# A two-block transformer kernel: a root of squares moved from the memory queries into a column factor, the opening put in another order, three sums regrouped

## What is computed

```
h    = rms_norm(x, mix_pre);   proj = h @ w_in            # two latents cq (384 wide), ckv (256 wide) among others
q    = rms_norm(cq, g_cq) @ w_uq;   kv = rms_norm(ckv, g_ckv) @ w_ukv
x    = x + rms_norm(mix @ w_mix_out, mix_post)
h    = rms_norm(x, mem_pre);   mem_n = rms_norm(mem, mem_kv)   # mem: 256 tokens, the same in both layers
q    = h @ w_q;   k, v = mem_n @ w_kv
p    = softmax(q @ k.T / 16)                              # 4 heads of 256 columns
x    = x + rms_norm((p @ v) @ w_o, mem_post)
x    = x + rms_norm(conv_ffn(rms_norm(x, ffn_pre)), ffn_post)
```

## Time and profile before

| what | us |
| --- | --- |
| median of 3 runs (2935.09 to 2936.07) | 2935.51 |
| the profiled execution | 2936.66 |
| its span, first to last instruction | 2934.9 |
| PE busy | 2823.6 |
| DVE busy | 1645.3 |
| ACT busy | 1175.8 |

### The profile page before, as it was taken

How to read it: one execution, slowest core, us unless ns; L and a number is a source line. 1 busy time by engine, 2 the same in 40 slices (tenths; PEclk the granted TensorE clock), 3 DMA queues, 4 the chain that set the end, 5 groups by cost and what they waited for, 6 DMA issues and landing times. The chain is left out here.

```text
span 2934.9 us, 35880 instructions
## 1 busy us (share of the span) xinstructions
PE 2823.6 (96%) x14736; PEld 2269.3 (77%) x14736; DVE 1645.3 (56%) x2278; ACT 1175.8 (40%) x1727; POOL 287.3 (10%) x249
## 2 busy tenths in 40 slices
PE   7999999999999999999999999999999999999998
PEld 3888777678878888786687878888786778788886
DVE  4467256676645443567753466653668663566643
ACT  3732434442243332434643343333435643443332
POOL 0110024310001110001200001100002101011100
PEclk8999999999999999999999999999999999999999
DMA  6200210045422222220032222232220132222231
GB/s 238 72 30 1 94 44 30 30 139 191 148 74 99 100 100 89 99 82 29 30 115 87 72 86 95 92 110 101 72 72 15 58 115 72 72 100 88 100 101 58
DMA packets 46003, 249.52 MB, mean 85 GB/s; under 512 B 5136, under 2 KB 7312, under 8 KB 19344
## 3 DMA queue, kind: packets, MB, share of 16 engines
q1 hardware_dynamic: 45840, 247.23, 24.5%
HBM read 245.11 MB, written 2.10 MB: 84 GB/s over the span
## 5 line engine op out<-in xcount | busy, mean ns | idle before, releaser
L271 DVE TENSOR_TENSOR ring_lo<-ring,ring_hi 128x2048 fp32r<-128x2048 f32 x199 | 457.2, 2298 | 552.9 <-ACT ring_hi L264 552.7
L322 PE MATMUL bank<-h_hi,ring_hi 128*128 128x512 f32 x1360 | 544.3, 400 | 12.5 <-PEq L380 8.7
L264 ACT ACTIVATE ring_hi<-ring 128x2048 fp32r<-128x2048 f32 x199 | 379.5, 1908 | 384.6 <-PE bank L322 356.6
L322 PE MATMUL bank<-h_hi,ring_lo 128*128 128x512 f32 x1360 | 531.5, 391 | 0.0
L1629 PE MATMUL bank<-h_hi,ring_hi 128*128 128x512 f32 x960 | 374.3, 390 | 0.0
L1633 PE MATMUL bank<-h_hi,ring_lo 128*128 128x512 f32 x960 | 373.5, 389 | 0.0
L1632 PE MATMUL bank<-h_lo,ring_hi 128*128 128x512 f32 x960 | 373.4, 389 | 0.0
L322 PEld LDWEIGHTS bank<-h_hi,ring_hi 128*128 128x128 f32 x1360 | 256.5, 189 | 70.3 <-DVE ring_lo L271 8.4
L322 PEld LDWEIGHTS bank<-h_hi,ring_lo 128*128 128x128 f32 x1360 | 256.3, 188 | 54.6
L322 PE MATMUL bank<-h_lo,ring_hi 128*128 128x512 f32 x624 | 244.9, 393 | 0.0
L1632 PEld LDWEIGHTS bank<-h_lo,ring_hi 128*128 128x128 f32 x960 | 180.2, 188 | 38.0 <-issue 0.5
(11 more groups left out here) (465 smaller groups left out, 4899.5 us busy)
## 6 DMA issues: line engine op xcount, KB each, us to landing
ring<-in_stream SPq DMA_DIRECT2D x199, 1024.0 KB, 4.9
mod_w<-in_stream SPq DMA_DIRECT2D x64, 256.0 KB, 3.6
ring<-in_stream SPq DMA_DIRECT2D x7, 512.0 KB, 4.1
ring<-in_stream SPq DMA_DIRECT2D x10, 256.0 KB, 4.2
h_spare<-in_stream SPq DMA_DIRECT2D x2, 1024.0 KB, 9.3
xT<-in_xT SPq DMA_DIRECT2D x2, 1024.0 KB, 18.1
xT<-in_xT SPq DMA_DIRECT2D x1, 2048.0 KB, 9.5
memT<-in_memT SPq DMA_DIRECT2D x2, 1024.0 KB, 5.3
```

Of the source, the lines that this page charges most:

```text
L264: nc.scalar.activation(self.slab_hi(slab + j), self.slab(slab + j), ACT.Copy).then_inc(slab_rounded, 1)
L271: nc.vector.tensor_tensor(lower, self.slab(slab + j), self.slab_hi(slab + j).bitcast(F32), ALU.subtract)\
L322: ins = nc.tensor.matmul(out, lhsT, rhs, start=start and w is w_hi and x is x_hi, stop=stop and w is w_lo)
```

## The change

It does six things in one kernel.

1. Opening: PE adds up `acc` and turns first, and sums the squares of x between the two halves of the third group. The slab roundings move: ACT rounds the first slab before the root of x, DVE halves it before it waits for `mod`. The second slab is rounded in the next block, behind the third rounded tile, and halved at tile 5, not 4.
2. Front: 5 useless products, not 18.
3. Latents: DVE adds the squares (three additions), PE does two products, not five.
4. Memory squares and their root are made in the first layer alone and kept in `mem_root`.
5. `mix_and_memory`: `h` is x times the gain, without the root. ACT makes `h_hi` from x, DVE `h_lo`; the squares go to `raw`; PE's eight sums are gone.
6. `memory_attention`: DVE adds the eight squares, PE sums them behind the first query tile, ACT takes the root, PE turns it into a column (four products of one column), and the exponential has it as a factor per partition. DVE multiplies each maximum by it.

```diff
@@ modulation: act @@
+                ws.round_to(act, WHOLE_SLABS, RING_SLABS)
                 act.wait_ge(x_summed.sem, x_summed.at(1))
                 root_of_mean(act, x_scales[:, 0, :], bank[:, 5, :])
                 row(2)
-                ws.round_to(act, WHOLE_SLABS + 1, RING_SLABS)
@@ front @@
-                linear("front", tiles, banks=6, busy=18, ...)
+                linear("front", tiles, banks=6, busy=5, ...)
@@ latents @@
+                    def low_totals(dve):
+                        for lo, hi, _, _ in latents:
+                            for n in range(lo + 1, hi):
+                                dve.wait_ge(low_squared.sem, low_squared.at(n + 1))
+                                if n > lo + 1:
+                                    dve.drain()
+                                last = nc.vector.tensor_tensor(low_square[lo], low_square[lo], low_square[n], ALU.add)
+                            last.then_inc(low_added.sem, 1)
@@ mix_and_memory: pe @@
-                for j in range(5):
+                for j in range(KT):
                     key_tile(j)
-                next_sums(range(4))
-                for j in range(5, KT - 1):
-                    key_tile(j)
-                next_sums(range(4, KT))
-                key_tile(KT - 1)
@@ mix_and_memory: act @@
+                for n in range(KT):
+                    key_out(n)
+                    round_h(n)
+                    if n % 2:
+                        ws.round_to(act, first_k + n // 2 + 2, ws.limit)
@@ mix_and_memory: dve @@
+                halves = {1: first_k + 2, 4: first_k + 3, 6: first_v}
+                for n in range(KT + 1):
+                    if n < KT:
+                        scaled(n)
+                    if n >= 1:
+                        split_h(n - 1)
+                    if n < KT:
+                        new_x(n)
+                    if n in halves:
+                        ws.halve_to(dve, halves[n], ws.limit)
@@ memory_attention: pe @@
+                pe.wait_ge(squares_added.sem, squares_added.at(1))
+                nc.tensor.matmul(bank[:, 7, :], con("ones"), total, start=True, stop=True).then_inc(square_summed.sem, 1)
...
+                pe.wait_ge(scale_ready.sem, scale_ready.at(1))
+                for tb in range(TB):
+                    last = nc.tensor.matmul(bank[:, 6, tb:tb + 1], scale[:, tb * P:(tb + 1) * P], con("ident", 1), start=True, stop=True)
@@ memory_attention: act, dve @@
                     nc.scalar.activation(probs[:, u % 2, 0:MEM], bank[:, 2 + u % 2, 0:MEM], ACT.Exp, bias=stat[:, u % 2, 0, 0:1],
-                                         accum_out=stat[:, u % 2, 1, 0:1]).then_inc(exp_done.sem, 1)
+                                         scale=column[:, u % TB:u % TB + 1], accum_out=stat[:, u % 2, 1, 0:1]).then_inc(exp_done.sem, 1)
...
+                        dve.drain()
+                        nc.vector.tensor_tensor(stat[:, u % 2, 0, 0:1], stat[:, u % 2, 0, 0:1], column[:, u % TB:u % TB + 1], ALU.mult)
```

More of the change, by code:

```diff
@@ L685, in scalar @@
                     self.square(act, 0, range(jobs[0]["tiles"]))
-                if self.halfway_scalar:
+                if self.halfway_scalar and not self.given:
                     self.halfway_scalar(act)
@@ L787, in build_program, with __init__ @@
         class PostNorm:
-            def __init__(self, gain, raw, squares, scales, by_pool=True, to=None, left=0):
+            def __init__(self, gain, raw, squares, scales, by_pool=True, to=None, left=0, alone=False):
                 if not by_pool:
@@ L946, in rope, with memory_attention @@
             stage(name, tensor=tensor, vector=vector, gpsimd=gpsimd)
-        def memory_attention(name, q, k, v, x, out, work):
+        def memory_attention(name, q, k, v, x, out, work, squares, total, scale, column):
             HEADS, N = KT // 2, KT // 2 * TB
@@ L1092, in vector @@
                 nc.vector.memset(stat[:, :, :, :], 0.0)
-                dve.drain()
+                for k in range(1, KT):
+                    if k > 1:
+                        dve.drain()
+                    last = nc.vector.tensor_tensor(total, total if k > 1 else squares[:, 0, :], squares[:, k, :], ALU.add)
+                last.then_inc(squares_added.sem, 1)
                 ws.halve_to(dve, AT_VALUE // SLAB, ws.limit)
+                dve.wait_ge(column_ready.sem, column_ready.at(1))
                 for u in range(N + 2):
@@ L1880, in mix_and_memory @@
             sub_normed = Signal("sub_normed", 2, shares="sum_read")
-            mem_squared = Signal("mem_squared", KT, shares="scored")
-            mem_summed = Signal("mem_summed", 1, shares="summed")
-            mem_scaled = Signal("mem_scaled", 1, shares="scaled")
+            mem_squared = Signal("mem_squared", KT if first else 0, shares="scored")
+            mem_summed = Signal("mem_summed", 1 if first else 0, shares="summed")
+            mem_scaled = Signal("mem_scaled", 1 if first else 0, shares="scaled")
             mem_normed = Signal("mem_normed", KT, shares="max_ready")
@@ L1964, in tensor @@
                 for n in range(TILES, KT):
-                    if n == TILES:
+                    if n == TILES and first:
                         for k in range(KT):
@@ L1969, in tensor @@
                         last.then_inc(mem_summed.sem, 1)
-                    if n == 7:
+                    if n == 7 and first:
                         pe.wait_ge(mem_scaled.sem, mem_scaled.at(1))
@@ L1999, in value_out, with round_h @@
                         nc.scalar.activation(v_out(0, tb), bank[:, v_banks[tb], :], ACT.Copy)
-                def next_squares(which):
-                    for n in which:
-                        act.wait_ge(added.sem, added.at(n + 1))
-                        if n >= SQUARES:
-                            act.wait_ge(post.next_square_summed.sem, post.next_square_summed.at(n - SQUARES + 1))
-                        nc.scalar.activation(post.squares[:, n % SQUARES, :], xT[:, AHEAD[n], :], ACT.Square)\
-                            .then_inc(post.next_square_ready.sem, 1)
-                def round_h(which):
-                    for k in which:
-                        act.wait_ge(h_normed.sem, h_normed.at(k + 1))
-                        nc.scalar.activation(h_hi[:, k, :], hT[:, k, :], ACT.Copy).then_inc(h_rounded.sem, 1)
+                def round_h(n):
+                    t = AHEAD[n]
+                    act.wait_ge(added.sem, added.at(n + 1))
+                    nc.scalar.activation(h_hi[:, t, :], xT[:, t, :], ACT.Identity, scale=h_gain(t)).then_inc(h_rounded.sem, 1)
+                    nc.scalar.activation(post.raw[:, t, :], xT[:, t, :], ACT.Square)
                 def upper(k):
@@ L2038, in scalar @@
                 act.wait_ge(sync.loaded.sem, sync.loaded.at(16))
-                for k in range(KT):
+                for k in range(KT if first else 0):
                     nc.scalar.activation(mem_squares[:, k, :], memT[:, k, :], ACT.Square).then_inc(mem_squared.sem, 1)
@@ L2045, in scalar @@
                         leave(n)
-                    if n == 3:
+                    if n == 3 and first:
                         act.wait_ge(mem_summed.sem, mem_summed.at(1))
@@ L2077, in vector, with scaled @@
             def vector(dve):
-                def new_x(n):
+                def scaled(n):
                     t = AHEAD[n]
@@ L2119, in vector @@
                     if n == 4:
-                        dve.wait_ge(mem_scaled.sem, mem_scaled.at(1))
+                        if first:
+                            dve.wait_ge(mem_scaled.sem, mem_scaled.at(1))
+                        else:
+                            dve.wait_ge(sync.loaded.sem, sync.loaded.at(16))
                         for k in range(KT + 2):
@@ L2873, in build_program @@
                            16: lambda pe: turn_rows(pe, (2, 3)), 17: lambda pe: turn_rows(pe, (4, 5))}
-                linear("front", tiles, banks=6, busy=18, sync=load_x, outs=outs, also=also, pe_also=pe_also, pool_also=gate_scan)
+                linear("front", tiles, banks=6, busy=5, sync=load_x, outs=outs, also=also, pe_also=pe_also, pool_also=gate_scan)
             probsT = tmp("probsT", [P, 2, 2 * ALLT], here)
```

123 lines of the change are left out of this document (50 added, 73 removed).

## The result

The changed kernel took 2921.37 us in the median of 5 executions (2912.87 to 2921.61), the kernel before 2935.60. The ratio on record is 0.9934, with a 95% interval of 0.9923 to 0.9944; it is not that of the two medians, which is 0.9952. The five executions lie in two groups, 2912.9 and 2914.3, and 2921.4 to 2921.6, and the median falls into the longer one. The profiled execution took 2912.87 (span 2911.1), 23.8 less than that of before. So the median gained 14.2 us and the profiled execution 23.8. There are two questions then: whether the steps of the prediction are what the trace shows, and why executions of one kernel lie 8 us apart.

What follows compares the result with a forecast made beforehand. The prediction took PE to bound the kernel, busy 2823.6 of 2934.9 us. Its terms summed to -21.0 us, from the median of 2935.5 to 2914.5, with an 8 in 10 range of 2905 to 2924.

Runs made afterwards that it cites:

- opening_filled: Changed kernel with slab steps sooner, POOL's addition later, useless products in PE's stands, also before the opening's third group and at the first projection's start: 2885.80 us.

## What to carry to other kernels

Before a wait is priced, check in the trace which buffer the awaited step fills: a product that starts ahead of the step's end doesn't need it. When sums are taken out of a queue that shares its helpers with weight preparation, move the preparation forward in the same edit, or the gain turns into waits for it. And compare versions with the stands of PE filled: a gain of some 25 us was read as 14 or 20 because of a clock that fell at places nobody had touched.

## What the runs showed of the hardware

- The clock fell at or behind stands of PE of 0.94 us (298), 1.73 (515), 1.89 (769) and 2.58 (2151) in one profile of the changed kernel and not in the other, at the same stand. All 35 stands of 3.05 to 5.80 us that the 14 profiles have from 20 us on had a low stretch behind them or over their end. The Trainium skill, TensorE: Matmul & The Clock Gate, section "What's actually happening", says that the gate's watching runs freely and isn't reset when a kernel starts. The two profiles of one program, with stretches at 298 and 517 us in one and at 772 in the other, are in keeping with it; no run here tests it.
- In opening_filled the clock fell at 26.1 us; in the 2.5 us before it PE did 16 records of one column and 8 of two, without a stand.
- Useless products ahead of real ones delay what is behind them if the clock is already low: 14 records took 3.24 us, where ten took 1.35 at the high clock.
- An exponential with a factor per partition takes 565 ns for 256 columns, without 474.
- POOL's addition of 896 columns takes 2.14 us with DVE idle, and is recorded with 3.0 to 3.9 where it starts beside a halving of DVE; in both it ends 1.95 behind the halving, and DVE's next step, recorded with 2.6, ends half a microsecond behind POOL. So the record of a step that had to wait contains the wait, and no idle time is shown.
